# The last expert job of a two-layer decoder trunk: taken out of the loop, and its result scattered by matmuls instead of through memory

## The reference

```python
def moe_swiglu(h, w_router, w1, w3, w2):
    logits = jnp.einsum('bsd,de->bse', h, w_router)
    top_v, top_i = lax.top_k(logits, 2)             # 2 of 8 experts for each token
    top_w = jax.nn.softmax(top_v, axis=-1)
    gate = jnp.sum(jax.nn.one_hot(top_i, 8) * top_w[..., None], axis=-2)
    y = jnp.zeros_like(h)
    for e in range(8):                              # w1, w3: 1024 x 3584, w2: 3584 x 1024
        y = y + gate[..., e:e + 1] * ((silu(h @ w1[e]) * (h @ w3[e])) @ w2[e])
    return y                                        # x = x + y is the output
```

## Time and profile before

| | |
|---|---|
| runs | 1542.56, 1537.78 and 1542.65 us, median 1542.56 |
| profiled execution | 1538.06 us |
| its span | 1536.2 us |
| PE, DVE, ACT, GpSimd busy | 97%, 80%, 67%, 1% of the span |
| granted TensorE clock, mean | 0.989 of full speed |
| DMA, from HBM and to it | 303 GB/s over the span |

### The profile page before, as it was taken

One profiled execution on the slowest core, in us unless ns is written; L12 is line 12 of the kernel. 1 busy time (PEld: TensorE's weight loads), 2 busy tenths in 40 slices (PEclk: granted clock), 3 DMA queues, 4 the chain that ended last, 5 costly groups with the idle time before them and its releaser, 6 DMA issues.

```text
span 1536.2 us, 21362 instructions
## 1 busy us (share of the span) xinstructions
PE 1493.8 (97%) x6973; PEld 1231.9 (80%) x6973; DVE 1227.3 (80%) x1152; ACT 1034.3 (67%) x1027; POOL 13.0 (1%) x17
## 2 busy tenths in 40 slices
PE   7999999999999999999999999999999999999994
PEld 6888888788888778888878878878888888888883
DVE  5885755445885769899899899889889989989987
ACT  5556544335556467787787687688778778778774
POOL 0000000000000010000000000000000000000000
PEclk9999999999999989999999999999999999999997
DMA  9953566257753399699999999999989989989985
GB/s 372 336 183 111 192 192 191 96 170 233 242 168 110 117 340 390 224 399 408 338 383 408 347 368 408 376 342 408 399 318 408 411 309 408 410 307 409 408 309 196
DMA packets 220188, 466.30 MB, mean 304 GB/s; under 512 B 14784, under 2 KB 40424, under 8 KB 220152
## 3 DMA queue, kind: packets, MB, share of 16 engines
q1 hardware_dynamic: 218432, 459.49, 81.3%
q0 software_dynamic: 1632, 6.33, 1.1%
q10 hardware_dynamic: 88, 0.02, 0.0%
HBM read 450.05 MB, written 15.73 MB: 303 GB/s over the span
## 4 chain that ended last, share of the span: by engine, by line
issue 63%; PE 34%; DVE 1%; DMA 1%; POOL 0%; ACT 0%; SPq 0%; POOLq 0%; ACTq 0%; DVEq 0%
PE bank L795 10%; PE bank L796 10%; PE bank L797 10%; PE bank L877 1%; DMA w_raw<-in_w_in 1%; PE bank L821 1%; PE bank L1096 0%; PE bank L861 0%; DMA x_scaled_rows<-y_by_slot,row_of_choice 0%; POOL x_by_slot L460 0%; PE bank L932 0%; PE bank L1009 0%; PE bank L849 0%; PE bank L912 0%; PE bank L940 0%
## 5 line engine op out<-in xcount | busy, mean ns | idle before, releaser
L1176 DVE TENSOR_TENSOR w_lo<-w_raw,w_hi 128x1024 fp32r<-128x1024 f32 (+1 forms) x448 | 778.5, 1756 | 104.5 <-ACT w_hi L491 86.6
L491 ACT ACTIVATE w_hi<-w_raw 128x1024 fp32r<-128x1024 f32 (+1 forms) x448 | 663.6, 1494 | 218.2 <-PE bank L797 174.2
L795 PE MATMUL bank<-w_hi,hT_hi 128*128 128x512 f32 (+1 forms) x1424 | 562.4, 395 | 7.0 <-DVE w_lo L1171 2.9
L796 PE MATMUL bank<-w_lo,hT_hi 128*128 128x512 f32 (+1 forms) x1424 | 553.1, 388 | 0.0
L797 PE MATMUL bank<-w_hi,hT_lo 128*128 128x512 f32 (+1 forms) x1424 | 553.0, 388 | 0.0
L795 PEld LDWEIGHTS bank<-w_hi,hT_hi 128*128 128x128 f32 x1424 | 268.3, 188 | 65.5 <-issue 7.3
L797 PEld LDWEIGHTS bank<-w_hi,hT_lo 128*128 128x128 f32 x1424 | 268.2, 188 | 56.3
L796 PEld LDWEIGHTS bank<-w_lo,hT_hi 128*128 128x128 f32 x1424 | 268.5, 189 | 51.9
L1171 DVE TENSOR_TENSOR w_lo<-w_raw,w_hi 128x2048 fp32r<-128x2048 f32 (+2 forms) x100 | 201.5, 2019 | 95.8 <-ACT w_hi L485 95.0
L485 ACT ACTIVATE w_hi<-w_raw 128x2048 fp32r<-128x2048 f32 (+2 forms) x100 | 169.8, 1700 | 160.3 <-PE bank L797 153.9
L795 PE MATMUL bank<-w_hi,hiddenM_hi 128*128 128x512 f32 x448 | 176.8, 395 | 2.3 <-DVE w_lo L1176 2.3
(11 more groups left out here) (232 smaller groups left out, 820.5 us busy)
## 6 DMA issues: line engine op xcount, KB each, us to landing
w_raw<-in_moe_w SPq DMA_DIRECT2D x672, 512.0 KB
w_raw<-in_w_in SPq DMA_DIRECT2D x64, 512.0 KB
w_raw<-in_dense_w SPq DMA_DIRECT2D x44, 512.0 KB
w_raw<-in_dense_w SPq DMA_DIRECT2D x44, 256.0 KB
w_raw<-in_w_out SPq DMA_DIRECT2D x16, 512.0 KB
x_by_slot<-x_residual SPq DMA_DIRECT2D x12, 512.0 KB, 11.2
w_raw<-in_w_pool_proj SPq DMA_DIRECT2D x8, 512.0 KB
w_raw<-in_w_attn_proj SPq DMA_DIRECT2D x8, 512.0 KB
```

The source lines that it names most:

```text
L491: act.activation(whi[:, m % SLOTS, 0:n], raw8[m % 8][:, 0:n], ACT.Copy).then_inc(s_hi, 1)
L795: pe.matmul(dst, ahi, bhi, start=start, stop=False)
L796: pe.matmul(dst, ahi, blo, start=False, stop=False)
L1176: dve.tensor_tensor(wlo[:, m % SLOTS, 0:n], raw8[m % 8][:, 0:n], whi[:, m % SLOTS, 0:n], ALU.subtract).then_inc(s_lo, 1)
```

## The change

The loop of PE, ACT and DVE runs over all jobs but one, and the body, now a function, is written once more behind it for the last job. In that copy:

- the four splits of the next job's chunks are left out on ACT and DVE, the eight small loads on SP, and the transposes and splits of the next job's x rows on all three engines; the load of those x rows into `x_slot_rows` stays;
- DVE works out, between up blocks, which tokens have a choice in the last job, a 0/1 matrix of slots against tokens (`selR`), gates for the last job and for the others, and the rows to gather (`last_rows`, `last_gates`, some 17 small instructions). PE transposes the matrix with two matmuls, ACT copies it to `selT`;
- y of the last job is not stored. When banks 6 and 7 are complete, ACT writes their rounded copy `yhi`, DVE the rest `ylo`, 128x512 each, PE multiplies `selT` with both (eight matmuls of 512 columns into four banks), and DVE adds the four results to x with the gate, 128x512 each;
- the rows of the other jobs are gathered as soon as SP has issued the last load and job 6's rows are stored. A token with one choice in the last job gathers its other choice's row in its place, with gate 0. The four additions stand in DVE's order behind its last split and ahead of the subtractions for `ylo`. They read from `y0`, `x_slot_rows` and `y_slot_rows`;
- the output is stored in four quarters of 256 KB.

Outside the last job: one more store of 512 KB in the first layer (17 for 16), one small DVE instruction in the job table, and one 128x128 copy by ACT ahead of the loop.

```diff
-            for k in range(SLOTS):
-                sp.wait_ge(s_lo, njobs * JOB_CHUNKS + (MOE0 + k - 8 + 1))
-                for j in range(2):
-                    sp.dma_start(raw8[k][:, 128 * j:128 * j + 128], A["moe_w2"][0, 0, 0:P, 0:P]).then_inc(s_ld[k], 16)
-            store_y(njobs - 1)
-            sp.wait_ge(s_ys, njobs * 16 + 16)
+            sp.wait_ge(s_ys, njobs * 16)
             sp.nop().then_inc(s_go, 1)
...
+            pool.wait_ge(s_rg, 1)
             pool.wait_ge(s_go, 1)
-            for t in range(TT):
-                for c in range(2):
+            for c in range(2):
+                for t in range(TT):
                     pool.indirect_dma_start(yg[c][t], None, yslot,
-                                            bass.IndirectOffsetOnAxis(rowu[:, c * TT + t:c * TT + t + 1], 0)
+                                            bass.IndirectOffsetOnAxis(rowg[:, c * TT + t:c * TT + t + 1], 0)
...
                 for k in range(20, 24):
                     split_m(d0 + k, HALF, j8)
-                for k in range(24, 27):
+                if last:
+                    for nh in range(2):
+                        act.wait_ge(s_yl, nh + 1)
+                        act.activation(yhi[:, 4 * nh:4 * nh + 4, :], bank[6 + nh][:].rearrange("p (k n) -> p k n", n=P),
+                                       ACT.Copy).then_inc(s_yhi, 1)
+                    return
+                for k in range(24, 28):
                     split_m(d0 + k, FULL, j8)
...
+            job(final, last=True)
+            pe.wait_ge(s_sts, 1)
+            for nh in range(2):
+                pe.wait_ge(s_ylo, nh + 1)
+                for t in range(TT):
+                    for y in (yhi, ylo):
+                        ins = pe.matmul(bank[2 + 2 * nh + t][:], selT[:, t * P:t * P + P], y[:, 4 * nh:4 * nh + 4, :],
+                                        start=(y is yhi), stop=(y is ylo))
+                    ins.then_inc(s_sca, 1)
...
+                    if last and b == 2:
+                        last_rows()
+                    if last and b == 3:
+                        last_gates()
...
+            job(final, last=True)
+            for c in range(2):
+                for t in range(TT):
                     dve.wait_ge(s_yg[c * TT + t], 16)
                     if c:
-                        dve.wait_ge(m_xa, 2 * t + 1)
-                    dve.scalar_tensor_tensor(X[:, t, :], yg[c][t], pr[:, 2 + c, t:t + 1], X[:, t, :],
+                        dve.wait_ge(m_xa, t + 1)
+                    dve.scalar_tensor_tensor(X[:, t, :], yg[c][t], egate[:, c, t:t + 1], X[:, t, :],
+                                             ALU.mult, ALU.add).then_inc(m_xa, 1)
+            for nh in range(2):
+                dve.wait_ge(s_yhi, nh + 1)
+                dve.tensor_tensor(ylo[:, 4 * nh:4 * nh + 4, :], bank[6 + nh][:].rearrange("p (k n) -> p k n", n=P),
+                                  yhi[:, 4 * nh:4 * nh + 4, :], ALU.subtract).then_inc(s_ylo, 1)
+            for nh in range(2):
+                for t in range(TT):
+                    dve.wait_ge(s_sca, 2 * nh + t + 1)
+                    dve.wait_ge(m_xa, TT + t + 1)
+                    v = X[:, t, 512 * nh:512 * nh + 512]
+                    dve.scalar_tensor_tensor(v, bank[2 + 2 * nh + t][:], lgate[:, t:t + 1], v,
                                              ALU.mult, ALU.add).then_inc(m_xa, 1)
```

More of the change, by code:

```diff
@@ L198, in build @@
         xn = sb("x_scaled_rows", [P, TT, D], F32, late)
-        yg = [[y[:, t, :] for t in range(TT)] for y in (y0, xn)]
+        yg = [[y0[:, t, :] for t in range(TT)], [xg[:], ysb[:]]]
         late.close()
@@ L332, in mixer_loads @@
                     c += 1
-                fill = [xslot[P * j:P * j + P, :] for j in range(NJ)] + [yslot[P * j:P * j + P, :] for j in range(E, NJ)]
+                fill = [xslot[P * j:P * j + P, :] for j in range(NJ)] + [yslot[P * j:P * j + P, :] for j in range(E - 1, NJ)]
                 for q, col in enumerate(ZCOL):
@@ L735, in _, with job @@
             act.wait_ge(s_tab, 1)
-            njobs = act.value_load(tabi[0:1, 15:16], min_val=E, max_val=NJ - 1)
+            final = act.value_load(tabi[0:1, 14:15], min_val=E - 1, max_val=NJ - 2)
             act.activation(silu0[:], cst[:, C_ONE:C_ONE + 1], ACT.Silu)
-            with act.Fori(0, njobs) as i:
+            act.activation(identR[:], ident, ACT.Copy).then_inc(s_idr, 1)
+            def job(i, last=False):
                 j8 = i * (JOB_CHUNKS // 8)
@@ L774, in _ @@
                     split_m(d0 + k, HALF, j8)
-                gathered_hi(i + 1)
+                if last:
+                    act.wait_ge(s_st, 1)
+                    act.activation(selT[:], bank[2][:, 0:S], ACT.Copy).then_inc(s_sts, 1)
+                else:
+                    gathered_hi(i + 1)
                 hid_hi_m(NB_E - 1, (NB_E - 1) % 2)
@@ L788, in _ @@
                     act.activation(ysb[:, 512 * j:512 * j + 512], bank[6 + j][:], ACT.Copy).then_inc(m_y, 1)
+            with act.Fori(0, final) as i:
+                job(i)
+            job(final, last=True)
         @block.tensor
@@ L1111, in _, with job @@
             pe.wait_ge(s_tab, 1)
-            njobs = pe.value_load(tabi[0:1, 15:16], min_val=E, max_val=NJ - 1)
-            with pe.Fori(0, njobs) as i:
+            final = pe.value_load(tabi[0:1, 14:15], min_val=E - 1, max_val=NJ - 2)
+            def job(i, last=False):
                 jd = JOB_CHUNKS // SLOTS
@@ L1139, in _ @@
                 up_block(NB_E - 1, i * jd + (NB_E - 1), 0)
-                gather(i + 1)
+                if last:
+                    pe.wait_ge(s_sel, 2)
+                    pe.wait_ge(s_idr, 1)
+                    for t in range(TT):
+                        ins = pe.matmul(bank[2][:, t * P:t * P + P], selR[:, t, :], identR[:], start=True, stop=True)
+                    ins.then_inc(s_st, 1)
+                else:
+                    gather(i + 1)
                 for k in range(KC_E):
@@ L1153, in _ @@
                         ins = three(bank[6 + nh][:], hidMhi[:, k, :], hidMlo[:, k, :], *w, k == 0, k == KC_E - 1)
-                    ins.then_inc(s_use, 1)
+                        if last and k == KC_E - 1:
+                            ins.then_inc(s_yl, 1)
+                    if not (last and k == KC_E - 1):
+                        ins.then_inc(s_use, 1)
+            with pe.Fori(0, final) as i:
+                job(i)
+            job(final, last=True)
[7 more added lines that the diff above has]
+                    ins.then_inc(s_sca, 1)
         @block.vector
@@ L1569, in _, with last_rows, last_gates, job @@
             dve.wait_ge(s_tab, 1)
-            njobs = dve.value_load(tabi[0:1, 15:16], min_val=E, max_val=NJ - 1)
-            with dve.Fori(0, njobs) as i:
+            final = dve.value_load(tabi[0:1, 14:15], min_val=E - 1, max_val=NJ - 2)
+            def last_rows():
+                row = rowf[:].rearrange("p (c t) -> p c t", t=TT)
+                chain(dve.tensor_scalar(lbase[:], tabf[:, 14:15], float(P), None, ALU.mult))
+                chain(dve.tensor_scalar(lrel[:], row, lbase[:], None, ALU.subtract))
+                dve.tensor_tensor(lpos[:], lrel[:, 0, :], lrel[:, 1, :], ALU.max)
+                chain(dve.tensor_scalar(lin[:], lrel[:], 0.0, None, ALU.is_ge))
+                for t in range(TT):
+                    ins = dve.tensor_scalar(selR[:, t, :], cst[:, C_IOTA:C_IOTA + P], lpos[:, t:t + 1], None, ALU.is_equal)
+                ins.then_inc(s_sel, 1)
+            def last_gates():
+                row = rowf[:].rearrange("p (c t) -> p c t", t=TT)
+                for c in range(2):
+                    ins = dve.tensor_tensor(lrow[:, c, :], row[:, 1 - c, :], row[:, c, :], ALU.subtract)
+                dve.tensor_tensor(egate[:], pr[:, 2:4, :], lin[:], ALU.mult)
+                chain(ins)
+                chain(dve.tensor_tensor(lrow[:], lrow[:], lin[:], ALU.mult))
+                chain(dve.tensor_tensor(lrow[:], lrow[:], row, ALU.add))
+                dve.tensor_copy(rowg[:], lrow[:].rearrange("p c t -> p (c t)")).then_inc(s_rg, 1)
+                chain(dve.tensor_tensor(lgate[:], egate[:, 0, :], egate[:, 1, :], ALU.add))
+                chain(dve.tensor_tensor(egate[:], pr[:, 2:4, :], egate[:], ALU.subtract))
+            def job(i, last=False):
                 j8 = i * (JOB_CHUNKS // 8)
@@ L1599, in _ @@
                     split_m(d0 + k, HALF, j8)
-                gathered_lo(i + 1)
+                if not last:
+                    gathered_lo(i + 1)
                 hid_lo_m(NB_E - 1, (NB_E - 1) % 2)
```

55 lines of the change are left out of this document (41 added, 14 removed).

## The result

The changed kernel took 1526.85 us (median of 4, 1526.59 to 1527.69) against 1542.61 for the kernel before (median of 4; the first three are those shown above, the fourth was 1542.68): ratio 0.9905, 95% interval 0.989 to 0.992, so 0.8 to 1.1% faster. The prediction was 1527.7, range 1523 to 1535.

A forecast was written before the change was run, and what follows sets the result against it. PE, busy in 97% of the span, was taken as the bound, except in a serial 20.9 us tail; 0.9 saved in the job and 11.7 in the tail gave 1525.5 or 1530.0 by level, middle 1527.7, range 1523 to 1535.

The forecast's parts named there:

- Outside the last job: Extra first-layer store of x, small DVE instruction and 128x128 copy on ACT: 0 each, at most 0.5 us together.
- The last job: Transposes replaced by two matmuls save 0.5 us, PE's stall 0.44; small DVE instructions cost 0; PE ends 0.9 earlier.
- The tail: Behind PE's last product: splits, store of y and gather behind it leave the serial chain; 11.7 us saved.
- subtractions for `ylo`: In the tail, behind four additions of 1.28 us each on DVE: two at 0.68, ending at 1517.1 and 1517.8.
- last addition: End of the scatter: DVE's four additions of 0.68 us, not PE's matmuls, set the pace from 1517.9 to 1520.6.
- late weights: Gathered rows share the DMA queue with the last weights: 0 to 1 us late for ACT, 0.3 taken.
- The clock term: PE's clock in the scatter, after standing still 2.8 us: full speed taken; at 1.2 GHz 1.1 us more.
- The output: Last quarter's store at the end: between 2.3 and 2.97 us, 2.7 taken, so the span ends at 1523.3.
- The gathers: GpSimd starts at about 1501.5, fourth lands at 1510.8, hidden by 4.3 us; other bound 0.7 late; 0 taken.
- GpSimd held up by DVE: Rival: GpSimd's gathers get nowhere until DVE finishes splitting at 1511.3; only 6.8 us saved, 1531.3 to 1535.8; chance 0.06.
- Instructions arriving late: Rival: fetching the copied last job stops PE, 10.5 us per stop; chance 0.03 for one, 0.03 for two.
- The change not doing what it says: Rival: the gather signal comes late, or additions and scatter last as long as the old chain, 20 us; chance 0.02.

The follow-up runs named there:

- e5: Changed kernel with the four additions of gathered rows cut from 1024 to 8 columns, leaving out nearly all other jobs' y: 1524.24 us.
- e6: Changed kernel with gathers signalled by ACT before up block 5 and the four additions moved among the splits of block 6 and the first chunks behind: 1524.47 us.
- e2: Changed kernel with ten idle matmuls behind the last product, so that PE does not stand still: 1526.16 us.
- e3: Changed kernel with the gathers starting only when y is complete, so nothing hides them: 1536.27 us.
- e8: Kernel before, unchanged, profiled again to catch an execution of the upper level: 1541.73 us.
- e9: Kernel before with only the change's 128x128 copy on ACT added ahead of the job loop: 1539.77 us beside 1541.44 without it.
- e10: Changed kernel with its 128x128 copy on ACT moved ahead of job 0's gathered rows, where it no longer delays the splits: 1529.6 us.
- e4: Changed kernel without the useless splits and loads, but the last job's y stored, gathered and added as before, output in two halves: 1534.9 us.
- e11: Changed kernel with early gathers and additions, plus DVE's split ahead of the job loop waiting for a signal behind GpSimd's four scatter issues: 1528.31 us.
- e7: Changed kernel with early gathers and additions, plus four idle matmuls behind the last product: 1524.55 us.

## Why the prediction was right, and where it was not

The mechanism of the tail was right and carries most of the gain. That the total came within 0.9 us of the forecast 1527.7 is partly luck, as shown under "Outside the last job". By its own steps, against the profiled execution of the changed kernel:

**The last job: 0.9 forecast, 1.2 measured.** From the start of the product ahead of the last job's first to the end of its last product it was 1515.30 - 1395.79 = 119.51 us before and is 1515.38 - 1397.09 = 118.29 now. The transposes and the stall of the earlier trace rows are gone. The small instructions of `last_rows` and `last_gates` stand in two groups, 1436.9 to 1438.0 and 1448.0 to 1449.1; DVE had caught up with ACT by 1464.5 and PE waited for none of it: cost 0, as said. The 0.3 us by which the job gained more than forecast was not followed.

**The tail: 11.7 forecast, 11.0 measured.** Counted from the last product's end:

| step ends at | forecast | measured |
|---|---|---|
| subtractions for `ylo` | 3.4 (1517.8 - 1514.4) | 2.9 (1518.28 - 1515.38) |
| last addition | 2.8 more | 3.9 more (1522.18) |
| end of the span | 2.7 more | 3.1 more (1525.3) |
| late weights | 0.3 | 0 |
| sum | 9.2 | 9.9 |

That DVE and not PE sets this tail held, and e5 and e6 show it from both sides: without the additions, or with them elsewhere, DVE waits for ACT and 2.4 to 2.6 us are gained. The first step was 0.5 too long in the forecast because it added full durations: the four additions take 4.9 us from the first's start to the last's end (4 x 1.28 is 5.1), the two subtractions end 1.2 behind that (1.4 forecast), each starting a little before the one ahead of it ends.

*The clock term failed.* "So I take full speed" went by the one fall that the trace of before had at its end. Here the clock fell 2.0 us after the last product, and e2 measures what that costs: the step of the last additions takes 3.0 us with PE kept busy (1520.61 - 1517.59) for 3.9 without, and the tail 9.2 for 9.9. The other bound had 1.1, with matmuls 0.46 apart; they were 0.43 apart.

*The output was longer.* "Half the bytes cannot be slower than 2.97" is refuted: 3.1 here and in e3, and 3.3 in the other traces with quarters, for example 1523.9 - 1520.61 (e2) and 1522.4 - 1519.15 (e6). Half the bytes in the last store did not shorten this time.

*The weights were not late.* ACT's splits from 1500 to 1512 wait for PE alone, 0.30 us each, eight times. The rows that share the queue with them cost 0, the lower bound. *The gathers* began at 1503.80, 2.3 us later than forecast (SP issued its last load by 1501.95, and GpSimd needed 1.85 from there), so the slack was 2.0 and not 4.3. The term stayed 0. Without any slack it is 9.4 (e3).

**Outside the last job: forecast 0, and the largest miss.** The step that failed is "0 each, at most 0.5 together", with "Nothing in one trace says which level comes out more often" beside it. The upper level is one chain of events (e8): full clock comes back some 2 us early at 555, so DVE's 2.29-us subtraction starts just ahead of GpSimd's fourth scatter, the scatter takes 2.93 for 0.95, its rows land late for the first job, PE stands 3.9 us for 1.8 and loses its clock. The copy on ACT delays the subtraction by 0.2 us, behind the scatter. Adding the copy to the kernel before takes the upper level away (e9), taking its effect from the changed kernel brings it back (e10). So against the lower level the change gives 1538.06 - 1526.85 = 11.2 us, and the other 4.6 of the 15.8 between the medians are the upper level that no longer comes (12 of 19 and 11 of 17 runs of the kernel before had it). The forecast of 12.6 for all levels was too much for one and too little for the other. The forecast was 1525.5 on the lower level and 1530.0 on the upper; the first was 1.35 too low, the second 3.15 too high, and the middle, 1527.7, came out close because these errors have opposite signs. That is luck, not a term that was known.

Against the lower level 12.6 were forecast and 10.95 came in the profiled pair: 0.7 less in the tail, 0.3 more in the job, and 1.3 less because the last job began at 1397.09 and not 1395.79. That pair compares unlike executions: the changed kernel's had the early clock, the one before the late clock. With the copy in place the early clock does not delay the scatter, but PE runs ahead, stands from 565.63 to 568.20 (2.57, 1.78 before) and is at half clock until 571.8. In e5, with the late clock, the last job began at 1395.57. Like against like the gain would be near 10.95 + 1.3 = 12.3 us with the late clock (an estimate, as no trace of the changed kernel itself has it), and it is 1541.73 - 1527.11 = 14.6 with the early one (e8).

**The chances.** By the prediction's own terms they don't add up: 0.86 and half of 0.06 make 0.89 for faster and not 0.91, and 0.03 and 0.05 make 0.08 for the same and not 0.06. Nothing else hangs on it.

**GpSimd held up by DVE (0.06)** did not decide, but its mechanism is real. Beside the last splits, 1.23 us each, an issue took 1.02 to 1.19 against 0.94 to 0.98 in the quiet tail of e3; beside splits of 2.29 it took 1.87 to 2.93. The Trainium skill (GPSIMD Engine Reference, section Key points) says that GpSimd contends with DVE's instructions of two SBUF inputs; the trace agrees, with 2.93 against 0.95 for the same scatter. Where the prediction went wrong is the place: it looked for the effect at the gathers, where the splits are short and the rows have slack, and not at the scatters of the earlier trace rows, which it had in hand and where the first job waits.

**Instructions arriving late (0.06)** falls. From 1395 to 1526 the trace has 4 and 5 instruction packets in two queues, so the copied job was fetched, but no matmul of it stands behind "issue".

**The change not doing what it says (0.02)** falls: the gathers land ahead of their use, and e4, where y takes the old way through memory, is 8.0 us slower.

## What to carry to other kernels

What a tail costs is read from its serial chain, and each half of a remedy can be priced alone: taking the useless splits out of ACT's way gave 3 us, keeping y out of memory with the gathers hidden another 8, and moving the last additions forward where DVE has time 2.4 more. When runs of one kernel fall on two levels, look for an event that a fraction of a microsecond decides before pricing an edit outside the path at nothing: compare two executions, one of each level, from the first instruction where they part, and look at the granted clock ahead of it. DVE work with two SBUF inputs that can start just ahead of GpSimd's DMA issues is such an event. And compare traces like with like: two profiled executions can differ by 1.3 us ahead of the part that was changed.

## What the runs showed of the hardware

- An indirect DMA of 128 rows took GpSimd 0.94 to 0.98 us to issue alone, 1.0 to 1.2 beside 128x1024 subtractions, and 2.6 to 2.9 when a 128x2048 subtraction of two SBUF inputs had begun just before it (e8, e10, e11). Begun together with the subtraction or 0.01 us ahead of it, it took 0.95 to 0.96 (changed kernel, e4, e6, e7). The first scatter, 2.33 beside a subtraction, took 1.03 without one (e11).
- A signal by a no-operation behind four indirect DMAs in GpSimd's order arrived before the third had been issued, by the profile's rows (e11: DVE went on at 557.76, the third issue began at 558.12).
- The granted clock fell 2.0 us after PE's last product in the changed kernel and 4.2 us after it before, and 5.3 us after it in e3 (1514.15 to 1519.46). The time from one trace was no forecast for the next.
- Around the router the granted clock came back to full at 554.4 to 557.2 us in 13 executions of nearly the same program, and without the copy on ACT the order of DVE and GpSimd 5 us later followed it (table under e8). At 568 us it stayed full where PE had stood for 1.69 to 1.84 us; where PE had stood for 2.16 to 4.42 it was at half when PE came back or 1.3 us later at most.
- From the last addition to the end, quarters of 256 KB took 3.1 to 3.3 us, and halves of 512 KB 2.97 before and 3.0 in e4.
